# Feed-forward up-projection: one 512-column matmul for both parts of the operand, the two sums added at read-out

## The chip, the core and the metric

The kernel runs on one core of a Trainium2 chip. The core has a matrix engine (PE, TensorE) that writes into PSUM (8 banks of 512 fp32 columns on 128 partitions), a vector engine (DVE), a scalar engine (ACT), a general one (POOL) and a queue (SP) that issues the weight transfers. Each engine works through its own instructions in order and waits on semaphores for the others. The metric is the device time of one execution in microseconds; lower is better.

## The reference

Two stacks of transformer-like layers on 256 tokens of width 1024: four layers (a mixer, cross attention, feed-forward, each with a layer norm) and two more (a mixer with memory attention, feed-forward, with RMS norms). Each of the six has the same kind of feed-forward stage, the part that matters here:

```
def causal_depthwise_conv(x, w, b):      # 3 taps along the sequence
    k_width = w.shape[0]
    s = x.shape[1]
    xp = jnp.pad(x, ((0, 0), (k_width - 1, 0), (0, 0)))
    y = xp[:, 0:s] * w[0]
    for k in range(1, k_width):
        y = y + xp[:, k:k + s] * w[k]
    return y + b

def conv_glu_ffn(x, w_up, conv_w, conv_b, w_down):   # w_up 1024 x 5632, w_down 2816 x 1024
    h = causal_depthwise_conv(x @ w_up, conv_w, conv_b)
    g, u = jnp.split(h, 2, axis=-1)
    return (jax.nn.silu(g) * u) @ w_down
```

The second stack's `conv_ffn` is the same with the halves exchanged. All is fp32.

## The kernel before

PE takes fp32r operands here, so every fp32 matrix is split into a high part (rounded to fp32r) and a low part (the remainder, fp32r again), and a product is three matmuls: high x high, high x low, low x high (`product`, L495). Activations lie transposed, features on partitions, as `xt[0]` (high) and `xt[1]` (low), each 8 tiles of 128 features x 256 tokens.

Weights stream in as 639 units of 128x1024 through a ring of 6 slots. For each unit ACT casts the raw weights to `w_hi` (L1027) and DVE subtracts to make `w_lo` (L1438). Both engines do this in `units`, which stands at fixed places of their programs and runs up to 4 units ahead of the unit in use. A cast waits until PE has used the unit six before.

A feed-forward stage has FT = 22 tiles q. A tile of up-projection is two units (128 features of each half), each 8 k-steps of `product` with the weight as the stationary and 256 tokens as the moving operand: 48 matmuls of 256 columns. Both halves of a tile share one PSUM bank, 4 for even and 6 for odd tiles (the first tile uses 4 and 5). From the third tile on PE follows each up-projection by the down-projection of tile q-2: 12 matmuls of 512 columns into banks 0 to 3 (L909), on the hidden tile in a high and a low part.

Between the two stands a round of ACT and DVE for each tile, both in program order:

- ACT (`tile`, L1346): casts of `units` (three from the third tile on), wait for the up-projection, two bias operations `qt = scale * sum + bias` (L1355, which is also the last of the three taps), SiLU (L1360) after DVE's taps of that half, `hid_hi` (L1365) after DVE's product.
- DVE (`tile`, L1880): the splits of the same units, wait for ACT's bias operations, four tap operations that read PSUM shifted by one or two tokens and add to `qt` (L1892), the product `kt` (L1901), `hid_lo` (L1904) after `hid_hi`.

The round begins again with ACT's cast after `hid_hi`. The bank of a tile is freed by the last tap operation. The order on each engine is that of the program; nothing is scheduled at build time.

Of the kernel before, what the change touches and what calls it, by code (L numbers as in the profile page):

```python
# [10 lines left out]
P = 128  # L11
# [82 lines left out]
class Memory:  # L94
    def __init__(self, nc, ctx, t):
# [4 lines left out]
        self.psum = ctx.enter_context(nc.psum_tensor("psum", [P, 8, BANK], F32))  # L100
        self.x_tok = sbuf("x_tok", [P, TB, D])
        self.n_tok = sbuf("n_tok", [P, TB, D])
        self.xt = [sbuf(f"xt_{part}", [P, KT, SEQ], F32R) for part in ("hi", "lo")]
        self.hid = [sbuf(f"hid_{part}", [P, 2, SEQ], F32R) for part in ("hi", "lo")]
        self.fresh = sbuf("fresh", [P, 2, 2, SEQ])
        self.gain_row = sbuf("gain_row", [P, D])
# [363 lines left out]
class Tensor(Engine):  # L470
# [24 lines left out]
    def product(self, out, stat, mov, first, last):  # L495
# [2 lines left out]
        self.eng.matmul(out, stat[0], mov[1], start=False, stop=False)  # L498
        return self.eng.matmul(out, stat[1], mov[0], start=False, stop=last)  # L499

    def operand(self, j, tb=slice(0, SEQ)):
        self.wait_ge("ready", self.x, j)
        return [x[:, j, tb] for x in self.m.xt]
# [376 lines left out]
    def feed_forward(self, params, silu_half):  # L880
        m = self.m
        bank = (4, 6)

        def up_tile(q):
            if q == 0:

                for k in (4, 5):
                    self.claim(k)
                units = [self.take(KT, P) for _ in range(2)]
                for k in range(KT):  # L890
                    for (hi, lo), b in zip(units, (4, 5)):
                        ins = self.product(m.psum[:, b, 0:SEQ], (hi[:, k, :], lo[:, k, :]), self.operand(k),
                                           k == 0, k == KT - 1)
                        if k == KT - 1:
                            self.used(ins, "made", self.tag, q)
            else:
                self.claim(bank[q % 2])
                for half in range(2):
                    self.used(self.feature_out(m.pair(bank[q % 2])[:, half, :], self.take(KT, P)),
                              "made", self.tag, q)  # L900
            self.free[bank[q % 2]] = ("conv", self.tag, q)
            if q == 0:
                self.free[5] = ("conv", self.tag, q)

        def down_part(q, unit, b, c, last):
            cs, tb = slice(c * BANK, (c + 1) * BANK), slice(b * P, (b + 1) * P)
# [111 lines left out]
class Scalar(Splitter):  # L1018
# [323 lines left out]
    def feed_forward(self, params, silu_half):  # L1342
# [2 lines left out]

        def tile(q):  # L1346
            s = q % 2
            out = [m.pair((4, 6)[s])[:, half, :] for half in range(2)]
            if q == 0:
                out = [m.psum[:, 4, 0:SEQ], m.psum[:, 5, 0:SEQ]]  # L1350
            self.wait_ge("made", self.tag, q)
            if q >= 2:
                self.wait_ge("prod", self.tag, q - 2)
            for half in range(2):
                ins = self.eng.activation(m.qt[:, 2 * s + half, :], out[half], ACT.Identity,  # L1355
                                          scale=col((TAPS - 1) * 2 * FT + half * FT + q),
                                          bias=col(TAPS * 2 * FT + half * FT + q))
            self.up(ins, "base", self.tag, q)
            self.wait_ge("gate_conv", self.tag, q)
            self.up(self.eng.activation(m.kt[:, s, :], m.qt[:, 2 * s + silu_half, :], ACT.Silu),  # L1360
                    "silu", self.tag, q)
            self.wait_ge("prod", self.tag, q)
            if q >= 2:
                self.wait_ge("down", self.tag, q - 2)
            self.up(self.eng.copy(m.hid[0][:, s, :], m.kt[:, 2 + s, :]), "hid_hi", self.tag, q)  # L1365
# [66 lines left out]
class Vector(Splitter):  # L1432
# [443 lines left out]
    def feed_forward(self, params, silu_half):  # L1876
# [2 lines left out]

        def tile(q):  # L1880
            s = q % 2
            out = [m.pair((4, 6)[s])[:, half, :] for half in range(2)]
            if q == 0:
                out = [m.psum[:, 4, 0:SEQ], m.psum[:, 5, 0:SEQ]]
            self.wait_ge("base", self.tag, q)
            first = []
            for d in range(1, TAPS):
# [305 lines left out]
```

## Time and profile before

| what | value |
|---|---|
| median of 3 runs | 2376.48 us (2375.91 to 2378.72) |
| profiled execution, its time | 2377.84 us |
| its span, first to last instruction | 2376.5 us |
| PE busy | 2130.2 us (90%) |
| DVE busy | 1615.2 us (68%) |
| ACT busy | 1217.9 us (51%) |
| matmuls | 13752 |
| mean granted PE clock | 0.945 of 2.4 GHz |

The profile is one execution. Matmuls overlap, so the distance between the starts of two of them, not their duration, is what one costs in a stream. "Idle before" names what released the engine. The line numbers are those of the kernel before.

### The profile page before, as it was taken

Reading aid. Unit: us, or ns where it says so; the run is one execution under the profiler, and the core shown is the slowest. Engines: PE = TensorE matmul, PEld = TensorE weight load, DVE = VectorE, ACT = ScalarE, POOL = GpSimd, SP = SyncE. Lnnn points to the kernel's source line nnn. Section 1 sums busy time; section 2 is a strip of 40 time slices with the busy share of each in tenths; the row PEclk is TensorE's granted clock in tenths of the full one; section 3 lists DMA queues with packets and bytes.
Section 4 is the critical chain, followed back from the end, with each engine's and each line's share of the span. In section 5 each row is a group of like instructions: output and inputs, shape, how many; then the busy total and the mean of one; then the engine's idle time right before and its main releaser. Section 6 shows DMA issues by size and latency. Waiting matters only on the chain.

```text
span 2376.5 us, 34303 instructions
## 1 busy us (share of the span) xinstructions
PE 2130.2 (90%) x13752; PEld 1932.7 (81%) x13752; DVE 1615.2 (68%) x2639; ACT 1217.9 (51%) x2105; POOL 180.3 (8%) x165
## 2 busy tenths in 40 slices
PE   8878899897899979889988787999788999888998
PEld 7757799796789978779987576998777999767997
DVE  4665777787577777577777656776565776766776
ACT  4444455483365555345545444554544655555554
POOL 3001200202010020220001012000000000000000
PEclk9998999898999989899998998999898999999999
DMA  9313566454366643346643134665422766423662
GB/s 286 123 54 113 157 195 185 122 166 140 111 184 187 178 130 124 124 128 200 186 161 128 54 129 144 188 186 151 138 81 86 209 186 185 136 89 116 199 187 94
DMA packets 435454, 352.90 MB, mean 148 GB/s; under 512 B 15869, under 2 KB 381750, under 8 KB 435296
## 3 DMA queue, kind: packets, MB, share of 16 engines
q1 hardware_dynamic: 429296, 332.49, 46.3%
q0 software_dynamic: 6000, 18.22, 2.2%
q8 instruction: 109, 1.79, 0.3%
q14 instruction: 49, 0.40, 0.1%
HBM read 349.62 MB, written 1.05 MB: 148 GB/s over the span
## 4 chain that ended last, share of the span: by engine, by line
PE 77%; DVE 12%; ACT 5%; issue 4%; POOL 1%; DMA 1%; ACTq 0%; SPq 0%; DVEq 0%; POOLq 0%
PE psum L497 19%; PE psum L498 18%; PE psum L499 18%; PE psum L909 14%; PE psum L815 2%; PE psum L802 2%; DVE xt_lo L1453 2%; DVE w_lo L1438 1%; DVE stat L1729 1%; DVE n_tok L1816 1%; PE psum L772 1%; DVE e L1724 1%; ACT xt_hi L1087 1%; POOL norm L2013 1%; ACT w_hi L1027 1%
## 5 line engine op out<-in xcount | busy, mean ns | idle before, releaser
L1438 DVE TENSOR_TENSOR w_lo<-w_raw,w_hi 128x1024 fp32r<-128x1024 f32 x639 | 751.4, 1224 | 193.8 <-ACT w_hi L1027 193.1
L497 PE MATMUL psum<-xt_hi,w_hi 128*128 128x256 f32 x2744 | 794.5, 290 | 70.2 <-ACT xt_hi L1087 50.3
L498 PE MATMUL psum<-xt_lo,w_hi 128*128 128x256 f32 x2744 | 791.7, 289 | 0.0
L499 PE MATMUL psum<-xt_hi,w_lo 128*128 128x256 f32 x2744 | 790.9, 288 | 0.0
L1027 ACT CAST w_hi<-w_raw 128x1024 fp32r<-128x1024 f32 x639 | 645.1, 1047 | 97.0 <-PE psum L499 71.9
L497 PEld LDWEIGHTS psum<-xt_hi,w_hi 128*128 128x128 f32 x2744 | 542.6, 198 | 81.0 <-ACT xt_hi L1087 54.5
L498 PEld LDWEIGHTS psum<-xt_lo,w_hi 128*128 128x128 f32 x2744 | 542.6, 198 | 4.4
L499 PEld LDWEIGHTS psum<-xt_hi,w_lo 128*128 128x128 f32 x2744 | 542.1, 198 | 0.0
L1892 DVE SCALAR_TENSOR_TENSOR qt<-psum,par,qt 128x255 f32<-128x255 f32 (+1 forms) x528 | 218.1, 476 | 152.1 <-ACT qt L1355 151.8
L497 PE MATMUL psum<-w_hi,xt_hi 128*128 128x512 f32 (+4 forms) x700 | 255.9, 366 | 20.5 <-ACT xt_hi L1087 11.6
L498 PE MATMUL psum<-w_lo,xt_hi 128*128 128x512 f32 (+4 forms) x700 | 253.3, 362 | 0.0
L499 PE MATMUL psum<-w_hi,xt_lo 128*128 128x512 f32 (+4 forms) x700 | 253.0, 361 | 0.0
L1355 ACT ACTIVATE qt<-psum,par 128x256 f32<-128x256 f32 x264 | 134.5, 560 | 197.4 <-PE psum L499 197.2
L909 PE MATMUL psum<-w_hi,hid_hi 128*128 128x512 f32 x528 | 207.7, 393 | 4.8 <-DVE hid_lo L1904 4.8
L909 PE MATMUL psum<-w_lo,hid_hi 128*128 128x512 f32 x528 | 207.0, 392 | 0.0
L909 PE MATMUL psum<-w_hi,hid_lo 128*128 128x512 f32 x528 | 205.4, 389 | 0.0
L2013 POOL TENSOR_TENSOR norm<-norm,eps_pow 128x1 f32<-128x1 f32 (+1 forms) x38 | 22.5, 592 | 2125.2 <-DVE norm L1806 1407.9
L497 PEld LDWEIGHTS psum<-w_hi,xt_hi 128*128 128x128 f32 x700 | 134.8, 193 | 42.4 <-ACT xt_hi L1087 12.5
L1078 ACT ACTIVATE fresh<-psum,par 128x256 f32<-128x256 f32 x71 | 35.7, 527 | 241.6 <-PE psum L566 184.7
L499 PEld LDWEIGHTS psum<-w_hi,xt_lo 128*128 128x128 f32 x700 | 134.9, 193 | 19.3
L498 PEld LDWEIGHTS psum<-w_lo,xt_hi 128*128 128x128 f32 x700 | 134.9, 193 | 18.7
L1360 ACT ACTIVATE kt<-qt 128x256 f32<-128x256 f32 x132 | 55.2, 418 | 182.2 <-DVE qt L1892 182.1
(223 smaller groups left out, 2197.5 us busy)
## 6 DMA issues: line engine op xcount, KB each, us to landing
w_raw<-in_f_w_up_dram SPq DMA_DIRECT2D x176, 512.0 KB, 5.1
w_raw<-in_f_w_down_dram SPq DMA_DIRECT2D x88, 512.0 KB, 5.0
w_raw<-in_w_up_dram SPq DMA_DIRECT2D x88, 512.0 KB, 4.9
w_raw<-in_w_down_dram SPq DMA_DIRECT2D x44, 512.0 KB, 5.1
w_raw<-in_x_w_q_dram SPq DMA_DIRECT2D x32, 512.0 KB, 4.6
w_raw<-in_x_w_o_dram SPq DMA_DIRECT2D x32, 512.0 KB, 4.9
w_raw<-in_a_w_qkv_dram SPq DMA_DIRECT2D x24, 512.0 KB, 4.6
w_raw<-in_w_in_fox_dram SPq DMA_DIRECT2D x20, 512.0 KB, 4.9
```

What stands on the lines that cost most here:

```text
L497: self.eng.matmul(out, stat[0], mov[0], start=first, stop=False)
L498: self.eng.matmul(out, stat[0], mov[1], start=False, stop=False)
L499: return self.eng.matmul(out, stat[1], mov[0], start=False, stop=last)
L802: ins = self.eng.transpose(m.psum[:, k, cols.start + b * P - q0:cols.start + (b + 1) * P - q0], m.e[:, g % 2, i, keys[b].start + c * P:key ...
L815: ins = self.eng.matmul(m.psum[p0:p0 + wide, k, slot * SEQ + q0:(slot + 1) * SEQ], vals(c), m.pt[:, g % 2, i, cols], start=c == 0, stop=c ...
L909: ins = self.eng.matmul(m.psum[:, 2 * b + c, :], stat[x], unit[y][:, 0, cs], start=False, stop=last and x == 1, skip_group_check=True)
L1027: self.up(self.eng.copy(self.m.hi[:, s, :], self.m.raw[:, s, :]), "w_hi", u)
L1355: ins = self.eng.activation(m.qt[:, 2 * s + half, :], out[half], ACT.Identity, scale=col((TAPS - 1) * 2 * FT + half * FT + q), bias=col(TA ...
L1360: self.up(self.eng.activation(m.kt[:, s, :], m.qt[:, 2 * s + silu_half, :], ACT.Silu), "silu", self.tag, q)
L1438: self.up(self.eng.tensor_tensor(self.m.lo[:, s, :], self.m.raw[:, s, :], self.m.hi[:, s, :].bitcast(F32), ALU.subtract), "w_lo", u)
L1453: n = self.up(self.eng.tensor_tensor(dst, src, hi.bitcast(F32), ALU.subtract), "ready", (tag, what), j)
L1892: ins = self.eng.scalar_tensor_tensor(cv[:, d:SEQ], out[half][:, 0:SEQ - d], col((TAPS - 1 - d) * 2 * FT + half * FT + q), cv[:, d:SEQ], A ...
```

## The change

Both parts of the operand move into one tile with the high and the low part of each k-tile side by side, so that they are one moving operand of 512 columns. The high part of the weight multiplies both in one matmul, which leaves two sums in one bank: the first 256 columns hold high x high, the other 256 high x low. The low part of the weight multiplies the operand's high part and adds to the first 256 columns. Each half of a tile now has a bank of its own (4 and 5, or 6 and 7). At read-out ACT copies the second sum of each half to SBUF (`low_part`), DVE adds the two sums into SBUF (`whole`), and both ACT's bias operations and DVE's taps read that instead of PSUM. The banks are freed by the adds.

```
+        self.xt_parts = sbuf("xt", [P, KT, 2, SEQ], F32R)
+        self.xt = [self.xt_parts[:, :, part, :] for part in range(2)]
...
+    def product_both(self, k, stat, j, first, last):
+        self.wait_ge("ready", self.x, j)
+        both = self.m.xt_parts[:, j]
+        self.eng.matmul(self.m.pair(k), stat[0], both, start=first, stop=False, skip_group_check=True)
+        return self.eng.matmul(self.m.pair(k)[:, 0, :], stat[1], both[:, 0, :], start=False, stop=last,
+                               skip_group_check=True)
...
         def up_tile(q):
+            ks = [bank[q % 2] + half for half in range(2)]
+            for k in ks:
+                self.claim(k)
+                self.free[k] = ("whole", self.tag, q)
...
             else:
-                self.claim(bank[q % 2])
-                for half in range(2):
-                    self.used(self.feature_out(m.pair(bank[q % 2])[:, half, :], self.take(KT, P)),
-                              "made", self.tag, q)
-            self.free[bank[q % 2]] = ("conv", self.tag, q)
+                for b in ks:
+                    hi, lo = self.take(KT, P)
+                    for k in range(KT):
+                        ins = self.product_both(b, (hi[:, k, :], lo[:, k, :]), k, k == 0, k == KT - 1)
+                    self.used(ins, "made", self.tag, q)
...
# ACT
-            out = [m.pair((4, 6)[s])[:, half, :] for half in range(2)]
+            out = [m.qt[:, 4 + 2 * s + half, :] for half in range(2)]
             self.wait_ge("made", self.tag, q)
             if q >= 2:
                 self.wait_ge("prod", self.tag, q - 2)
+            for half in range(2):
+                ins = self.eng.copy(m.kt[:, 4 + 2 * s + half, :], m.pair(4 + 2 * s + half)[:, 1, :])
+            self.up(ins, "low_part", self.tag, q)
+            self.wait_ge("whole", self.tag, q)
...
# DVE
-            out = [m.pair((4, 6)[s])[:, half, :] for half in range(2)]
+            out = [m.qt[:, 4 + 2 * s + half, :] for half in range(2)]
+            self.wait_ge("low_part", self.tag, q)
+            for half in range(2):
+                ins = self.eng.tensor_tensor(out[half], m.pair(4 + 2 * s + half)[:, 0, :],
+                                             m.kt[:, 4 + 2 * s + half, :], ALU.add)
+            self.up(ins, "whole", self.tag, q)
             self.wait_ge("base", self.tag, q)
```

What each engine has in a row for the third tile (q = 2) of the first stage. ACT before, from the casts to the next cast (L1355 are the bias operations):

```order
L1027 CAST w_hi<-w_raw 128x1024 [waits w_landed0]
L1027 CAST w_hi<-w_raw 128x1024 [waits w_landed1]
L1027 CAST w_hi<-w_raw 128x1024 [waits w_used,w_landed2]
L1355 ACTIVATE qt<-psum,par 128x256 [waits w_used]
L1355 ACTIVATE qt<-psum,par 128x256
```

ACT after (L1365 are now the copies, L1369 the bias operations, L1374 SiLU, L1379 `hid_hi`):

```order
L1039 CAST w_hi<-w_raw 128x1024 [waits w_landed0]
L1039 CAST w_hi<-w_raw 128x1024 [waits w_landed1]
L1039 CAST w_hi<-w_raw 128x1024 [waits w_used,w_landed2]
L1365 COPY kt<-psum 128x256 [waits w_used]
L1365 COPY kt<-psum 128x256
L1369 ACTIVATE qt<-qt,par 128x256 [waits whole]
L1369 ACTIVATE qt<-qt,par 128x256
L1374 ACTIVATE kt<-qt 128x256 [waits gate_conv]
L1379 CAST hid_hi<-kt 128x256 [waits w_used,prod]
```

The two copies took the place of the bias operations behind PE's signal, and the bias operations moved behind a wait for DVE. DVE at the same tile, before:

```order
L1438 TENSOR_TENSOR w_lo<-w_raw,w_hi 128x1024 [waits w_hi] x3
L1892 SCALAR_TENSOR_TENSOR qt<-psum,par,qt 128x255 [waits base]
L1892 SCALAR_TENSOR_TENSOR qt<-psum,par,qt 128x255
L1892 SCALAR_TENSOR_TENSOR qt<-psum,par,qt 128x254 [waits vec] x2
L1901 TENSOR_TENSOR kt<-kt,qt 128x256 [waits conv,silu]
L1904 TENSOR_TENSOR hid_lo<-kt,hid_hi 128x256 [waits hid_hi]
```

and after (L1899 are the adds, L1909 the taps):

```order
L1452 TENSOR_TENSOR w_lo<-w_raw,w_hi 128x1024 [waits w_hi] x3
L1899 TENSOR_TENSOR qt<-psum,kt 128x256 [waits low_part]
L1899 TENSOR_TENSOR qt<-psum,kt 128x256
L1909 SCALAR_TENSOR_TENSOR qt<-qt,par 128x255 [waits base]
L1909 SCALAR_TENSOR_TENSOR qt<-qt,par 128x255
L1909 SCALAR_TENSOR_TENSOR qt<-qt,par 128x254 [waits vec] x2
L1918 TENSOR_TENSOR kt<-kt,qt 128x256 [waits conv,silu]
L1921 TENSOR_TENSOR hid_lo<-kt,hid_hi 128x256 [waits hid_hi]
```

Two adds with a wait for ACT went in ahead of the wait for the bias operations.

## Rows read from the trace of the kernel before

**Rows 1.** The page's part 1: busy time, share of span, instructions.
```profile
PE 2130.2 (90%) x13752; PEld 1932.7 (81%) x13752; DVE 1615.2 (68%) x2639; ACT 1217.9 (51%) x2105; POOL 180.3 (8%) x165
```

**Rows 2.** Windows, of tiles in the first feed-forward stage and of cross attention.
```profile
core 0: us, PE busy (x) PEld busy (x) DVE busy (x) ACT busy (x) POOL busy (x), PEclk, DMA share, GB/s
298.00:445.00 147.00, 147.00 (x1043) 138.66 (x1042) 104.03 (x156) 83.89 (x122) 0.00 (x0) 1.00 0.62 185
606.00:660.00 54.00, 43.15 (x198) 34.85 (x197) 29.88 (x49) 19.05 (x37) 10.24 (x6) 0.93 0.25 69
```

**Rows 3.** PE's timeline over a tile: start us, us, line, operation.
```profile
293.73 0.40 PE L909 MATMUL psum<-w_hi,hid_hi 128*128 128x512 f32 x1
...
296.48 0.28 PE L497 MATMUL psum<-xt_hi,w_hi 128*128 128x256 f32 x1
...
302.23 0.40 PE L909 MATMUL psum<-w_hi,hid_hi 128*128 128x512 f32 x1
```

**Rows 4.** ACT's timeline of a tile in the middle of the stage.
```profile
297.52 3.14 ACT L1027 CAST w_hi<-w_raw 128x1024 fp32r<-128x1024 f32 x3
302.44 1.02 ACT L1355 ACTIVATE qt<-psum,par 128x256 f32<-128x256 f32 x2 [1.77 <-PE psum L499]
```

**Rows 5.** DVE's timeline of the same tile.
```profile
298.59 3.50 DVE L1438 TENSOR_TENSOR w_lo<-w_raw,w_hi 128x1024 fp32r<-128x1024 f32 x3 [0.52 <-ACT w_hi L1027]
303.49 1.65 DVE L1892 SCALAR_TENSOR_TENSOR qt<-psum,par,qt 128x255 f32<-128x255 f32 x4 [1.40 <-ACT qt L1355]
```

**Rows 6.** DVE's timeline at the start of the first stage.
```profile
270.22 4.63 DVE L1438 TENSOR_TENSOR w_lo<-w_raw,w_hi 128x1024 fp32r<-128x1024 f32 x4 [0.26 <-ACT w_hi L1027]
274.97 1.66 DVE L1892 SCALAR_TENSOR_TENSOR qt<-psum,par,qt 128x255 f32<-128x255 f32 x4
...
277.63 0.43 DVE L1904 TENSOR_TENSOR hid_lo<-kt,hid_hi 128x256 fp32r<-128x256 f32 x1 [0.47 <-ACT hid_hi L1365]
...
284.46 3.50 DVE L1438 TENSOR_TENSOR w_lo<-w_raw,w_hi 128x1024 fp32r<-128x1024 f32 x3 [0.53 <-ACT w_hi L1027]
287.87 1.65 DVE L1892 SCALAR_TENSOR_TENSOR qt<-psum,par,qt 128x255 f32<-128x255 f32 x4
...
291.48 3.50 DVE L1438 TENSOR_TENSOR w_lo<-w_raw,w_hi 128x1024 fp32r<-128x1024 f32 x3 [0.53 <-ACT w_hi L1027]
```

**Rows 7.** ACT's timeline of the third tile, beside rows 6.
```profile
283.38 2.94 ACT L1027 CAST w_hi<-w_raw 128x1024 fp32r<-128x1024 f32 x3
286.23 1.01 ACT L1355 ACTIVATE qt<-psum,par 128x256 f32<-128x256 f32 x2
```

**Rows 8.** Prices: DVE's timeline, groups by shape (busy us, mean ns), ACT's timeline.
```profile
87.00 0.41 DVE L1523 TENSOR_TENSOR swap<-psum,rope_sin 128x256 f32<-128x256 f32 x1
87.33 0.41 DVE L1524 TENSOR_TENSOR swap<-psum,rope_sin 128x256 f32<-128x256 f32 x1
...
L1438 DVE TENSOR_TENSOR w_lo<-w_raw,w_hi 128x1024 fp32r<-128x1024 f32 x639 | 751.4, 1224 | 193.8 <-ACT w_hi L1027 193.1
L1525 DVE TENSOR_TENSOR tok<-tok,swap 128x256 f32<-128x256 f32 x12 | 5.1, 425 | 0.4
L1522 DVE TENSOR_TENSOR tok<-psum,rope_cos 128x256 f32<-128x256 f32 x12 | 5.0, 420 | 0.4 <-PE psum L499 0.3
...
L1278 ACT ACTIVATE e<-e,stat 128x256 f32<-128x256 f32 x64 | 31.5, 493 | 0.0
L1278 ACT ACTIVATE e<-psum,stat 128x256 f32<-128x256 f32 x48 | 22.2, 477 | 19.9 <-DVE stat L1737 19.9
L1033 ACT COPY v<-psum 128x256 f32<-128x256 f32 x8 | 2.6, 377 | 12.0 <-PE psum L499 12.0
...
510.41 1.71 ACT L1171 ACTIVATE pt<-v,small 128x256 f32<-128x256 f32 x4
```

**Rows 9.** DVE's timeline: last tile of the first, first and last of the fifth stage.
```profile
450.64 0.42 DVE L1904 TENSOR_TENSOR hid_lo<-kt,hid_hi 128x256 fp32r<-128x256 f32 x1 [0.47 <-ACT hid_hi L1365]
...
1843.38 0.43 DVE L1904 TENSOR_TENSOR hid_lo<-kt,hid_hi 128x256 fp32r<-128x256 f32 x1 [0.47 <-ACT hid_hi L1365]
...
2014.54 0.42 DVE L1904 TENSOR_TENSOR hid_lo<-kt,hid_hi 128x256 fp32r<-128x256 f32 x1 [0.47 <-ACT hid_hi L1365]
```

**Rows 10.** PE's timeline at the end of the first stage.
```profile
451.12 0.50 PE L909 MATMUL psum<-w_hi,hid_hi 128*128 128x512 f32 x1 [0.80 <-DVE hid_lo L1904]
```

More of the change, by code:

```diff
@@ L58 @@
     "base",
+    "low_part",
     "silu", "hid_hi",
@@ L71 @@
     "vec",
+    "whole",
     "gate_conv", "conv", "prod", "hid", "final",
@@ L102, in __init__ @@
         self.n_tok = sbuf("n_tok", [P, TB, D])
-        self.xt = [sbuf(f"xt_{part}", [P, KT, SEQ], F32R) for part in ("hi", "lo")]
+        self.xt_parts = sbuf("xt", [P, KT, 2, SEQ], F32R)
+        self.xt = [self.xt_parts[:, :, part, :] for part in range(2)]
         self.hid = [sbuf(f"hid_{part}", [P, 2, SEQ], F32R) for part in ("hi", "lo")]
@@ L884, in up_tile @@
         def up_tile(q):
+            ks = [bank[q % 2] + half for half in range(2)]
+            for k in ks:
+                self.claim(k)
+                self.free[k] = ("whole", self.tag, q)
             if q == 0:
-                for k in (4, 5):
-                    self.claim(k)
                 units = [self.take(KT, P) for _ in range(2)]
                 for k in range(KT):
-                    for (hi, lo), b in zip(units, (4, 5)):
-                        ins = self.product(m.psum[:, b, 0:SEQ], (hi[:, k, :], lo[:, k, :]), self.operand(k),
-                                           k == 0, k == KT - 1)
+                    for (hi, lo), b in zip(units, ks):
+                        ins = self.product_both(b, (hi[:, k, :], lo[:, k, :]), k, k == 0, k == KT - 1)
                         if k == KT - 1:
@@ L896, in up_tile @@
             else:
-                self.claim(bank[q % 2])
-                for half in range(2):
-                    self.used(self.feature_out(m.pair(bank[q % 2])[:, half, :], self.take(KT, P)),
-                              "made", self.tag, q)
-            self.free[bank[q % 2]] = ("conv", self.tag, q)
-            if q == 0:
-                self.free[5] = ("conv", self.tag, q)
+                for b in ks:
+                    hi, lo = self.take(KT, P)
+                    for k in range(KT):
+                        ins = self.product_both(b, (hi[:, k, :], lo[:, k, :]), k, k == 0, k == KT - 1)
+                    self.used(ins, "made", self.tag, q)
         def down_part(q, unit, b, c, last):
@@ L1347, in tile @@
             s = q % 2
-            out = [m.pair((4, 6)[s])[:, half, :] for half in range(2)]
-            if q == 0:
-                out = [m.psum[:, 4, 0:SEQ], m.psum[:, 5, 0:SEQ]]
+            out = [m.qt[:, 4 + 2 * s + half, :] for half in range(2)]
             self.wait_ge("made", self.tag, q)
@@ L1881, in tile @@
             s = q % 2
-            out = [m.pair((4, 6)[s])[:, half, :] for half in range(2)]
-            if q == 0:
-                out = [m.psum[:, 4, 0:SEQ], m.psum[:, 5, 0:SEQ]]
+            out = [m.qt[:, 4 + 2 * s + half, :] for half in range(2)]
[4 more added lines that the diff above has]
+            self.up(ins, "whole", self.tag, q)
             self.wait_ge("base", self.tag, q)
```

## The prediction

> **What bounds the kernel now.** I read the page's busy shares first: PE is busy for 2130 of 2376.5 us, the other engines much less [rows 1]. An average says little about the six feed-forward stages, so next come the windows. Over 147 us in the middle of the first one PE is busy all the time at a granted clock of 1.00 (its upper level, 2.4 GHz), DVE for 104.0 and ACT for 83.9 us [rows 2]. PE's timeline shows the same tile by tile: 12 down-projection matmuls of 512 columns from 293.73 to 296.48, then 48 up-projection matmuls of 256 columns until 302.23, with no gap [rows 3]. That is 2.75/12 = 0.229 us for 512 columns and 5.75/48 = 0.120 us for 256, and 8.50 us a tile. ACT sits idle for 1.77 us waiting for PE before it reads a tile [rows 4], and DVE then waits 1.40 us for ACT [rows 5]. So each tile ends when PE does.
>
> The start of the same stage shows the second limit. There PE is ahead (the first two tiles carry no down-projection), DVE has no such wait, and its tiles follow at 291.48 - 284.46 = 7.02 us [rows 6]. This is what the round between DVE and ACT costs by itself: three splits, four tap operations, the product, the low part of the hidden tile, and ACT's operations between them. The slack between the two limits is 8.50 - 7.02 = 1.48 us a tile. I expect the change to use up more than that, so it is to be judged on this round, not on PE.
>
> **PE's part.** Per tile, 16 pairs of 256-column matmuls become 16 matmuls of 512 columns; the other 16 of 256 columns stay. Columns are unchanged; what goes is a weight load and the fixed share of a matmul, 2 x 0.120 - 0.229 = 0.011 us each [rows 3]. PE's tile becomes 16 x (0.229 + 0.120) + 2.75 = 8.33 us, a gain of 0.17. Two banks per tile are claimed instead of one; both are freed after the two adds, before the taps, where they used to be held until after the taps, so no new wait comes from there. The new layout of the operand changes strides, not sizes, of the writes of its two parts; I cost it at nothing (these writes come before the loop of tiles).
>
> **ACT's part.** New are two copies of 128x256 out of PSUM, before the two bias operations. A copy of this size takes 0.377 us [rows 8]; two in a row some 0.7. In the start regime ACT's three casts begin at 283.38 and its bias operations at 286.23 [rows 7], while DVE's taps begin at 287.87 [rows 6]. A wait-free ACT would thus finish the copies by 286.95, about 0.9 us before DVE has ended its splits. They are hidden there, and cost nothing. What would expose them is a tile that PE finishes late, and by the sum below PE is not late. Queued behind the copies is ACT's wait for the adds; that delays nothing that DVE is not itself delaying.
>
> **DVE's part, and the new wait.** Two adds of 128x256 (PSUM and SBUF in, SBUF out) stand between the splits and the taps. Two such operations out of PSUM follow each other at 87.33 - 87.00 = 0.33 us and the second takes 0.41 [rows 8]: 0.74 us. Only then may ACT start the two bias operations. They used to run while DVE was still splitting; now DVE stands and waits for them. Their price: 1.02 us for the pair when they read PSUM [rows 4]; now they read SBUF. Exponentials of 256 elements took 0.493 us from SBUF and 0.477 from PSUM [rows 8], so I add 0.02 each: 1.06. Each handoff costs what lies between the end of ACT's pair, 302.44 + 1.02 = 303.46, and DVE's start, 303.49 [rows 4, 5]: 0.03, twice. The taps now read SBUF instead of PSUM; a DVE operation on 256 elements took 0.420 us from PSUM and 0.425 from SBUF [rows 8], so they stay at 1.65.
>
> Added to the round: 0.74 + 0.03 + 1.06 + 0.03 = **1.86 us**. The round becomes 7.02 + 1.86 = 8.88 us, above PE's 8.33, so DVE and ACT set the pace and PE gets to wait about 0.55 us a tile. It will wait before the second half of a tile's up-projection, since that weight's split is the first in DVE's batch of three and the one on which PE has the least lead.
>
> **The sum.** The first tile: DVE ended its splits at 270.22 + 4.63 = 274.85 and its taps began at 274.97 [rows 6]. The new taps begin at 274.85 + 1.86 = 276.71: 1.74 later. The second tile carries two splits; a split is (3.50 - 1.22)/2 = 1.14 us in a row of them [rows 5, 8], so its round was 7.02 - 1.14 = 5.88 and becomes 7.74. Twenty more rounds follow at 8.88: 177.6. From the old start of the first hid_lo to the new start of the last: 1.74 + 7.74 + 177.6 = 187.1 us. Before, this was 450.64 - 277.63 = 173.0 in the first stage and 2014.54 - 1843.38 = 171.2 in the fifth, which is the shortest [rows 6, 9]; the others took 172.5 to 173.0, and the six together are 1035.4. What PE does after the last hid_lo (it waited 0.80 us for it and then had the last seven groups to do [rows 10]) is the same in both kernels. Sum: 6 x 187.1 - 1035.4 = **+87 us**. The profiled execution took 2377.8 against the median's 2376.5; from the median this gives **2463.5 us**, 3.7% slower.
>
> Ends for the unknowns. Low: bias pair as two scaled operations from SBUF in a row of four, 1.71 us for four, which is 0.41 + 0.49 = 0.90 [rows 8]; taps at the 0.33 pitch of plain operations, 3 x 0.33 + 0.41 = 1.40, or 0.25 less; added 1.45, round 8.47, six stages 6 x (1.33 + 7.33 + 169.4) = 1068, so +33 us: 2409.5. High: adds without overlap 0.84, bias pair without overlap 1.12, added 2.02, round 9.04, six stages 1143.6, so +108 us: 2485.
>
> **Rivals.** *Shorter taps.* DVE might read SBUF faster than PSUM. The rows speak against it (0.420 and 0.425 [rows 8]), but none is of this operation. With 0.25 us less per tile the round is 8.63, a stage 1.49 + 7.49 + 172.6 = 181.6, and the time 2376.5 + 6 x 181.6 - 1035.4 = 2431. The Trainium skill, VectorE: DVE Perf Modes, in the section on the TRN2 errata, has 58 fixed cycles for VectorE from SBUF against 120 from PSUM, and 224 against 172 for ScalarE. By that rule, an estimate: four taps save 4 x 62 cycles at 0.96 GHz, 0.26 us, and the two bias operations lose 0.09; on ACT's pair of 1.02 the added time is 0.74 + 0.06 + 1.11 - 0.26 = 1.65, the round 8.67, and the time about 2436. The durations in rows 8 bear out the second half in sign and not the first.
>
> *PE stays the bound, and the kernel is faster.* If the round stayed under PE's 8.33, the 0.17 us would be gained on 132 tiles: -23 us, 2353. It decides at the round: no change in the time needs 6 x (22c - 8.28) = 1035.4 with c the round, which is c = 8.22, or 1.20 us added where I have 1.86. The adds and two handoffs are 0.80; the bias pair would have to take 0.4 us with unchanged taps. Even the low end, 1.45, does not reach it. Against it too: the 7.02 us rounds with which each stage starts are lost whatever PE does.
>
> *The 512-column matmul doesn't save its share.* If the two sums in one bank cost PE as much as before, PE's tile stays at 8.50, still under 8.88, and the time is the forecast's. This matters only beside the low end.
>
> *PE's clock falls.* PE now pauses in every tile. In the window of cross attention it was busy for 43 of 54 us and still had 0.93 of the clock [rows 2]; with 94% busy I expect 1.00. If it fell to the lower level in a stretch, PE's tile would double there, about 8 us lost per tile so hit; one tile a stage gives +50 on top, 2510.
>
> **Chances.** Forecast (rounds 8.75 to 9.05) 0.63, shorter taps 0.18, PE remains the bound 0.06, between that and no change 0.05, clock or another stall 0.08. The range has to hold forecast, shorter taps and both ends: 2405 to 2490. A measurement here can tell about 0.2% from no change. Faster by over 0.2% 0.06, within 0.2% 0.04, slower 0.90.
>
> **What would show it.** DVE's timeline: adds right behind the splits without a wait on the copies, then an idle stretch of about 1.12 us for ACT's bias operations in every tile, and hid_lo at 8.88 us from the third tile on instead of 7.0 and then 8.50. ACT: no wait for PE before the copies, a wait for the adds instead. PE: a pause of some 0.55 us a tile for the split weights, 0.349 us for a pair of 512 and 256 columns. It would be wrong if the copies showed up as what DVE waits for, if the bias pair took well under 1 us, or if PE had no pause.

## The result, and the profile after

| what | before | changed kernel |
|---|---|---|
| median on the same chip | 2376.30 us | 2480.66 us (2478.77 to 2481.71, 4 runs) |
| ratio | | 1.0436, 95% interval 1.0418 to 1.0454 |
| profiled execution: its span | 2376.5 us | 2479.2 us |
| mean granted PE clock | 0.945 | 0.935 |

The kernel is 4.4% slower. The forecast was 2463.5 us, 3.7% slower, with a range of 2405 to 2490.

The page's part 1 of the changed kernel, to be read beside [rows 1]:

```profile
PE 2159.2 (87%) x11640; PEld 1824.2 (74%) x11640; DVE 1706.8 (69%) x2903; ACT 1290.2 (52%) x2369; POOL 180.3 (7%) x165
```

PE has 2112 instructions fewer and yet is busy for 29 us more. That is no work: matmuls overlap, so a pause shows as idle time only once the last record has ended. The first matmul after a pause has a longer record (0.50 us instead of 0.40, below), and where the clock is low every record is longer (0.63 us, below). The chain of work that ended last has changed owner. The page's part 4 of the kernel before:

```profile
PE 77%; DVE 12%; ACT 5%; issue 4%; POOL 1%; DMA 1%; ACTq 0%; SPq 0%; DVEq 0%; POOLq 0%
```

and of the changed kernel:

```profile
DVE 42%; PE 32%; ACT 18%; issue 6%; POOL 1%; DMA 1%; ACTq 0%; SPq 0%; DVEq 0%; POOLq 0%
```

The window over the middle of the first feed-forward stage, as in [rows 2] (columns: window, us, then PE, weight load, DVE, ACT, POOL busy with instructions, granted clock, DMA share, GB/s), and one over the end of that stage:

```profile
298.00:445.00 147.00, 142.20 (x725) 117.47 (x726) 109.64 (x180) 86.98 (x149) 0.00 (x0) 1.00 0.59 178
466.00:474.00 8.00, 7.37 (x21) 5.57 (x21) 7.21 (x12) 1.44 (x2) 0.56 (x1) 0.69 0.23 67
```

In the middle PE was busy for all 147 us before; now it is idle for 4.8 us of them, at the same full clock. It is starved there, not slowed. (4.8 us in 147/8.95 = 16.4 tiles are 0.29 each; by the starts of the matmuls a pause is longer.)

DVE's timeline of the changed kernel, from the first tile of the first stage and then a tile in the stage; it answers [rows 5] and [rows 6]:

```profile
269.39 4.63 DVE L1452 TENSOR_TENSOR w_lo<-w_raw,w_hi 128x1024 fp32r<-128x1024 f32 x4 [0.25 <-ACT w_hi L1039]
...
275.86 1.67 DVE L1909 SCALAR_TENSOR_TENSOR qt<-qt,par 128x255 f32<-128x255 f32 x4 [1.16 <-ACT qt L1369]
277.98 0.43 DVE L1918 TENSOR_TENSOR kt<-kt,qt 128x256 f32<-128x256 f32 x1 [0.46 <-ACT kt L1374]
278.88 0.43 DVE L1921 TENSOR_TENSOR hid_lo<-kt,hid_hi 128x256 fp32r<-128x256 f32 x1 [0.47 <-ACT hid_hi L1379]
...
286.69 0.43 DVE L1921 TENSOR_TENSOR hid_lo<-kt,hid_hi 128x256 fp32r<-128x256 f32 x1 [0.47 <-ACT hid_hi L1379]
287.64 3.50 DVE L1452 TENSOR_TENSOR w_lo<-w_raw,w_hi 128x1024 fp32r<-128x1024 f32 x3 [0.52 <-ACT w_hi L1039]
291.05 0.75 DVE L1899 TENSOR_TENSOR qt<-psum,kt 128x256 f32<-128x256 f32 x2
292.97 1.67 DVE L1909 SCALAR_TENSOR_TENSOR qt<-qt,par 128x255 f32<-128x255 f32 x4 [1.16 <-ACT qt L1369]
...
296.59 3.50 DVE L1452 TENSOR_TENSOR w_lo<-w_raw,w_hi 128x1024 fp32r<-128x1024 f32 x3 [0.52 <-ACT w_hi L1039]
```

One round is 296.59 - 287.64 = 8.95 us. The adds follow the splits with no wait on the copies. Then DVE is idle for 1.16 us, released by ACT's bias operations. From the adds' start to the taps' start it is 292.97 - 291.05 = 1.92 us, which was nothing before; from the taps to the next splits it is 296.59 - 292.97 = 3.62, against 291.48 - 287.87 = 3.61 in [rows 6]. So the whole addition sits at that one place. The second tile's hid_lo comes 286.69 - 278.88 = 7.81 us after the first's.

ACT's timeline at the same tile, which answers [rows 4] and [rows 7]:

```profile
289.42 0.63 ACT L1365 COPY kt<-psum 128x256 f32<-128x256 f32 x2
291.84 1.09 ACT L1369 ACTIVATE qt<-qt,par 128x256 f32<-128x256 f32 x2 [1.79 <-DVE qt L1899]
```

The copies end at 289.42 + 0.63 = 290.05, a full 1.00 us before DVE's adds begin. The bias pair now waits 1.79 us for DVE, where it waited 1.77 for PE in [rows 4].

PE's timeline at a tile in the middle, which answers [rows 3]:

```profile
321.39 0.39 PE L510 MATMUL psum<-xt,w_hi 128*128 128x512 f32 x1
...
324.71 0.50 PE L510 MATMUL psum<-xt,w_hi 128*128 128x512 f32 x1 [0.35 <-DVE w_lo L1452]
...
327.59 0.39 PE L921 MATMUL psum<-w_hi,hid_hi 128*128 128x512 f32 x1
```

The up-projection takes 327.59 - 321.39 = 6.20 us with one pause in the middle, before the second half's first matmul, for the split weight. Eight pairs without a pause took 327.59 - 324.71 = 2.88 us (a first one that starts slower included).

Four operations by their source lines (engine, operation, count, duration in ns as least/median/most). The taps and the bias operations of the kernel before:

```profile
L1892 DVE SCALAR_TENSOR_TENSOR qt<-psum,par,qt x528: 469/474/486, 275.0 to 2360.6; 128x255 f32<-128x255 f32 x88, 128x254 f32<-128x254 f32 x88
...
L1355 ACT ACTIVATE qt<-psum,par x264: 547/558/568, 273.9 to 2358.9; 128x256 f32<-128x256 f32 x132
```

and of the changed kernel, with the copies, what they waited for and what waited for them:

```profile
L1909 DVE SCALAR_TENSOR_TENSOR qt<-qt,par x528: 474/479/486, 275.9 to 2461.4; 128x255 f32<-128x255 f32 x88, 128x254 f32<-128x254 f32 x88
...
L1369 ACT ACTIVATE qt<-qt,par x264: 584/596/607, 274.7 to 2459.6; 128x256 f32<-128x256 f32 x132
...
L1365 ACT COPY kt<-psum x264: 355/368/381, 272.9 to 2457.3; 128x256 f32<-128x256 f32 x132
its engine sat idle before it (us, times) until:
  PE psum L511: 3.4, 3
who waited for it (us, times):
  DVE qt L1899: 0.7, 1
```

Taps from SBUF take 479 ns against 474 from PSUM, bias operations 596 against 558. The copies waited for PE in 3 of 132 tiles, 3.4 us in all. DVE's adds waited for the copies once, 0.7 us, in the first tile of the last stage; there the sums come late in the kernel before too (DVE waited 1.13 us for the bias operations).

**The sum against the spans.** The changed span is 102.7 us longer. The six stretches from a stage's first hid_lo to its last were 1035.4 us and are now 1118.1 (186.7 five times and 184.5 in the last stage), which is +82.7. The first round of each lasts 7.80 to 7.82, the other twenty 8.93 to 8.96; the exception is the final round of the last stage, 6.66, where no weights are left to split. The other +20.0 us lie between the stages: from a last hid_lo to the next first one, and the two ends of the kernel. The forecast had 6 x (7.74 + 177.6) - 1035.4 = +76.6 for the first and 6 x 1.74 = +10.4 for the second.

PE's timeline at the end of the first stage, which answers [rows 10]:

```profile
458.92 0.47 PE L921 MATMUL psum<-w_hi,hid_hi 128*128 128x512 f32 x1 [3.11 <-DVE w_lo L1452]
...
466.06 0.80 PE L921 MATMUL psum<-w_hi,hid_hi 128*128 128x512 f32 x1 [6.21 <-DVE hid_lo L1921]
466.66 0.63 PE L921 MATMUL psum<-w_lo,hid_hi 128*128 128x512 f32 x1
467.08 0.63 PE L921 MATMUL psum<-w_hi,hid_lo 128*128 128x512 f32 x1
...
473.04 0.40 PE L921 MATMUL psum<-w_hi,hid_lo 128*128 128x512 f32 x1
```

Before, PE waited 0.80 us for the last hid_lo; now it waits 3.11 and 6.21 us, and then its matmuls of 512 columns start 467.08 - 466.66 = 0.42 us apart instead of 0.23, until 470.92. The granted clock of that window is 0.69 (above): the lower level, 1.2 GHz, for its first half. The last of these 21 matmuls starts 7.46 us after hid_lo where it was 5.15 before; over the six stages it starts 13.0 us later in all (1.6 to 2.8 each). In the other stages the first wait is 3.1 to 3.2 us too, and the second is 5.5 to 6.0, in the last stage 3.25.

### The profile page after: what moved, and what is told of

It is laid out like the page before. It is cut to its first block, busy times and chain, and to the rows that moved or that the text cites. A ratio compares the mean times of both kernels' runs of the same rounds, so it can differ in the third digit from the quotient of the medians.

```text
span 2479.2 us, 30607 instructions
## 1 busy us (share of the span) xinstructions
PE 2159.2 (87%) x11640; PEld 1824.2 (74%) x11640; DVE 1706.8 (69%) x2903; ACT 1290.2 (52%) x2369; POOL 180.3 (7%) x165
## 4 chain that ended last, share of the span: by engine, by line
DVE 42%; PE 32%; ACT 18%; issue 6%; POOL 1%; DMA 1%; ACTq 0%; SPq 0%; DVEq 0%; POOLq 0%
DVE w_lo L1452 19%; PE psum L501 8%; PE psum L502 7%; PE psum L503 7%; DVE qt L1909 7%; ACT w_hi L1039 6%; ACT qt L1369 6%; DVE qt L1899 3%; DVE kt L1918 2%; ACT kt L1374 2%; PE psum L828 2%; DVE xt L1467 2%; PE psum L815 2%; PE psum L921 1%; DVE stat L1743 1%
## 5 line engine op out<-in xcount | busy, mean ns | idle before, releaser
L510 PE MATMUL psum<-xt,w_hi 128*128 128x512 f32 x2112 | 775.6, 407 | 63.7 <-DVE w_lo L1452 38.5
L511 PE MATMUL psum<-xt,w_lo 128*128 128x256 f32 x2112 | 596.8, 283 | 0.0
L510 PEld LDWEIGHTS psum<-xt,w_hi 128*128 128x128 f32 x2112 | 403.3, 191 | 191.7 <-DVE w_lo L1452 64.7
L511 PEld LDWEIGHTS psum<-xt,w_lo 128*128 128x128 f32 x2112 | 405.0, 192 | 4.4
L1909 DVE SCALAR_TENSOR_TENSOR qt<-qt,par 128x255 f32<-128x255 f32 (+1 forms) x528 | 220.1, 479 | 153.5 <-ACT qt L1369 153.5
L501 PE MATMUL psum<-w_hi,xt 128*128 128x512 f32 (+4 forms) x700 | 256.4, 366 | 21.1 <-ACT xt L1099 11.6
L1369 ACT ACTIVATE qt<-qt,par 128x256 f32<-128x256 f32 x264 | 144.5, 594 | 238.9 <-DVE qt L1899 238.9
L502 PE MATMUL psum<-w_lo,xt 128*128 128x512 f32 (+4 forms) x700 | 253.6, 362 | 0.0
L503 PE MATMUL psum<-w_hi,xt 128*128 128x512 f32 (+4 forms) x700 | 253.2, 362 | 0.0
L501 PE MATMUL psum<-xt,w_hi 128*128 128x256 f32 x632 | 191.1, 302 | 39.5 <-ACT xt L1099 25.5
L502 PE MATMUL psum<-xt,w_hi 128*128 128x256 f32 x632 | 188.7, 299 | 0.0
L503 PE MATMUL psum<-xt,w_lo 128*128 128x256 f32 x632 | 188.3, 298 | 0.0
L501 PEld LDWEIGHTS psum<-w_hi,xt 128*128 128x128 f32 x700 | 135.2, 193 | 42.7 <-ACT xt L1099 12.5
L501 PEld LDWEIGHTS psum<-xt,w_hi 128*128 128x128 f32 x632 | 131.8, 209 | 43.5 <-ACT xt L1099 27.8
L921 PEld LDWEIGHTS psum<-w_hi,hid_hi 128*128 128x128 f32 x528 | 102.7, 194 | 80.3 <-DVE hid_lo L1921 36.2
```

Source lines behind the costliest of these rows:

```text
L501: self.eng.matmul(out, stat[0], mov[0], start=first, stop=False)
L510: self.eng.matmul(self.m.pair(k), stat[0], both, start=first, stop=False, skip_group_check=True)
L511: return self.eng.matmul(self.m.pair(k)[:, 0, :], stat[1], both[:, 0, :], start=False, stop=last, skip_group_check=True)
L921: ins = self.eng.matmul(m.psum[:, 2 * b + c, :], stat[x], unit[y][:, 0, cs], start=False, stop=last and x == 1, skip_group_check=True)
L1909: ins = self.eng.scalar_tensor_tensor(cv[:, d:SEQ], out[half][:, 0:SEQ - d], col((TAPS - 1 - d) * 2 * FT + half * FT + q), cv[:, d:SEQ], A ...
```

## The experiments

**The two halves of the change apart.** The first kernel has the joined matmul but reads only the first sum, as the kernel before did; the second has the read-out with the matmuls split again.

```
# e1_matmul_alone: ACT and DVE as before, on the first sum alone
-            out = [m.qt[:, 4 + 2 * s + half, :] for half in range(2)]
+            out = [m.pair(4 + 2 * s + half)[:, 0, :] for half in range(2)]
...
-                ins = self.eng.copy(m.kt[:, 4 + 2 * s + half, :], m.pair(4 + 2 * s + half)[:, 1, :])
-            self.up(ins, "low_part", self.tag, q)
-            self.wait_ge("whole", self.tag, q)
...
# e2_readout_alone: 48 matmuls of 256 columns
-        self.eng.matmul(self.m.pair(k), stat[0], both, start=first, stop=False, skip_group_check=True)
+        for part in range(2):
+            self.eng.matmul(self.m.pair(k)[:, part, :], stat[0], both[:, part, :], start=first and part == 0,
+                            stop=False, skip_group_check=True)
```

> PE's part alone: the joined matmuls stay, but the second sum is not read; ACT's bias operations and DVE's taps read the first sum from PSUM as in the kernel before, the banks are freed after the taps (so the product high weight x low operand is left out of the result). Theory A (the round of DVE and ACT costs the time, PE's part saves 0.17 us a tile): tiles at 8.33 us, 132 x 0.176 = 23 us faster than before, 2353 us. Rival B (the joined matmul, the second bank or the new layout of the operand carries part of the loss): at or above 2376 us, tiles at 8.50 us or more.

> The read-out alone: two banks, copies, adds and waits as in the changed kernel, but the joined matmul of 512 columns is issued as two of 256 columns, one into each half of the bank, so that PE's tile is 8.50 us again. Theory A: PE at 8.50 is still under the round of 8.95, so nothing changes against the changed kernel, 2480 us within 3. Rival B (PE's part matters): 0.17 us x 132 = 23 us slower than the changed kernel, 2503 us.

Measured: the matmul alone 2366.51 us, ratio 0.9953 (0.9938 to 0.9968); the read-out alone 2478.96 us, 1.0428 (1.0413 to 1.0444). The same window of the first:

```profile
298.00:445.00 147.00, 147.00 (x774) 125.39 (x774) 105.57 (x158) 84.90 (x123) 0.00 (x0) 1.00 0.63 188
```

and of the second:

```profile
298.00:445.00 147.00, 144.27 (x999) 133.36 (x998) 110.23 (x180) 87.99 (x149) 0.00 (x0) 1.00 0.59 174
```

With the matmul alone PE is busy for the whole window, and a round takes 8.38 to 8.39 us: the joined matmul saves 0.11 us a tile, 14.1 us in the six stretches (1021.3 against 1035.4). In the time only 9.9 us of that arrive; no run shows where the rest goes. With the read-out alone the rounds are 8.95, the same as in the changed kernel, though 2.73 us of the 147 are left idle instead of 4.80. So the whole loss is the read-out's, and what the matmul saves is not seen beside it. My 2353 for the first was too low: the saving is smaller than my 0.17, and three or four of the 21 rounds of a stage, those at its start, never wait for PE.

**The bias operations taken out of the path.** They read the first sum from PSUM as before, beside the splits; the adds stay on DVE.

```
-            out = [m.qt[:, 4 + 2 * s + half, :] for half in range(2)]
+            out = [m.pair(4 + 2 * s + half)[:, 0, :] for half in range(2)]      # ACT
...
-            self.up(ins, "low_part", self.tag, q)
-            self.wait_ge("whole", self.tag, q)
...
-            self.wait_ge("low_part", self.tag, q)                               # DVE
+            self.wait_ge("base", self.tag, q)
```

> All work of the changed kernel stays, but ACT's two bias operations read the first sum from PSUM straight behind the copies and do not wait for DVE's adds (so the product high weight x low operand is missing from the last tap); DVE's adds wait for the bias operations instead, and the taps follow the adds. Theory A (what costs is that DVE stands while ACT makes the bias operations, 1.16 us a tile, beside 0.75 us of adds): round 8.95 - 1.16 + 0.05 = 7.8 us, under PE's 8.33, so PE is the bound again and the time is about 2355 to 2360 us. Rival C (the two adds and the two copies as work are what costs, the order is not): near 2480 us, at least above 2430.

Measured: 2374.03 us (2370.65 to 2377.25), 0.9988 (0.9978 to 0.9997). DVE's timeline of a tile:

```profile
293.72 3.50 DVE L1450 TENSOR_TENSOR w_lo<-w_raw,w_hi 128x1024 fp32r<-128x1024 f32 x3 [0.53 <-ACT w_hi L1039]
297.14 0.75 DVE L1897 TENSOR_TENSOR qt<-psum,kt 128x256 f32<-128x256 f32 x2
297.92 1.67 DVE L1908 SCALAR_TENSOR_TENSOR qt<-qt,par 128x255 f32<-128x255 f32 x4
...
301.54 2.36 DVE L1450 TENSOR_TENSOR w_lo<-w_raw,w_hi 128x1024 fp32r<-128x1024 f32 x2 [0.52 <-ACT w_hi L1039]
```

The round is 301.54 - 293.72 = 7.82 us: the adds stay at 0.75, the 1.16 us of idle time are gone, and later in each stage PE sets 8.39. ACT's pair behind DVE's adds is thus worth 1.13 us a tile by itself, and without that wait the time is about that of before (this kernel leaves high x low out of the last tap). The time is above the expected 2355 to 2360. The stretches sum to 1021.9 us, which is 13.5 less than before, where 16 to 21 were expected of the time, since PE's tile is 8.39 and not 8.33, and part of that is lost again between the stages. PE's timeline at the end of the first:

```profile
448.89 0.50 PE L921 MATMUL psum<-w_hi,hid_hi 128*128 128x512 f32 x1 [2.16 <-DVE hid_lo L1920]
```

The wait is 2.16 us instead of 0.80, the granted clock of 448 to 456 us is 0.79, and in four of the six stages the last matmul starts 6.74 to 6.78 us after hid_lo instead of 5.15.

**The price of the adds, and of the copies.** Each is done twice, the extra result going to a spare tile.

```
# e5_adds_twice, on DVE
+                self.eng.tensor_tensor(m.v[:, s, half * SEQ:(half + 1) * SEQ], m.pair(4 + 2 * s + half)[:, 0, :],
+                                       m.kt[:, 4 + 2 * s + half, :], ALU.add)
# e7_copies_twice, on ACT
+                self.eng.copy(m.v[:, s, half * SEQ:(half + 1) * SEQ], m.pair(4 + 2 * s + half)[:, 1, :])
```

> The changed kernel with DVE's two adds issued twice (the first pair into a spare tile). A dose of one of the two terms. Theory A (everything DVE does in the round counts in full): 2 x 0.33 = 0.67 us more a tile, round 9.61 us, 132 tiles: 88 us above the changed kernel, 2569 us. Rival D (part of the adds is cover for the wait on ACT or on PE): well under 88 us more.

> The changed kernel with ACT's two copies out of PSUM issued twice (the first pair into a spare tile), 0.55 us more work for ACT a tile. Theory A says that the copies end about 1.0 us before DVE has its splits, so that another 0.55 us hides too: 2480 us within 3. Rival F (the copies are on the path): 132 x 0.55 = 73 us more, 2553 us.

Measured: adds twice 2567.41 us, 1.0799 (1.0784 to 1.0813), with rounds of 9.61 us; copies twice 2481.26 us, 1.0436 (1.0422 to 1.0451), with rounds of 8.95. DVE's timeline with the adds doubled:

```profile
299.63 3.49 DVE L1452 TENSOR_TENSOR w_lo<-w_raw,w_hi 128x1024 fp32r<-128x1024 f32 x3 [0.53 <-ACT w_hi L1039]
303.04 0.75 DVE L1899 TENSOR_TENSOR v<-psum,kt 128x256 f32<-128x256 f32 x2
303.71 0.74 DVE L1902 TENSOR_TENSOR qt<-psum,kt 128x256 f32<-128x256 f32 x2
...
309.23 2.36 DVE L1452 TENSOR_TENSOR w_lo<-w_raw,w_hi 128x1024 fp32r<-128x1024 f32 x2 [0.53 <-ACT w_hi L1039]
```

and ACT's with the copies doubled:

```profile
299.97 0.63 ACT L1365 COPY v<-psum 128x256 f32<-128x256 f32 x2
300.50 0.65 ACT L1367 COPY kt<-psum 128x256 f32<-128x256 f32 x2
302.39 1.09 ACT L1371 ACTIVATE qt<-qt,par 128x256 f32<-128x256 f32 x2 [1.25 <-DVE qt L1901]
```

0.67 us more of adds lengthens the round by 0.66; 0.53 us more of copies lengthens nothing, it only shortens ACT's wait for DVE from 1.79 to 1.25 us. The path and its cover are where the prediction put them.

**The ends of the stages.** PE gets 24 matmuls on a tile of zeros, into a bank that is free there, before its last wait for hid_lo; in the second kernel also 12 before the wait for the split weights. The third is the changed kernel again, on the same chip as the second.

```
# e9_both_waits_filled; e6_end_filled has the second loop alone, with its own claim
+        self.claim(4)
+        for _ in range(12):
+            self.eng.matmul(m.psum[:, 4, :], m.zeros[:, 0:P], m.zeros[:], start=True, stop=True, skip_group_check=True)
         units = [self.take(1, D) for _ in range(2)]
...
+                    if (b, c, q) == (0, 0, FT - 1):
+                        for _ in range(24):
+                            self.eng.matmul(m.psum[:, 4, :], m.zeros[:, 0:P], m.zeros[:], start=True, stop=True,
+                                            skip_group_check=True)
                     self.wait_ge("hid", self.tag, q)
```

> The changed kernel with 24 extra matmuls of 512 columns on zeros into the free bank 4 at the end of each stage, where PE waits 6.2 us for the last hidden tile and its clock then falls to 1.2 GHz for the first 11 of 21 down-projection matmuls (0.43 against 0.23 us). Theory E (the wait lets the clock fall, and that carries part of the about 8 us between the stages that the rounds don't explain): the 21 matmuls take 4.8 instead of 7.2 us, and 5 to 8 us less than the changed kernel in all, about 2474 us; granted clock up. If the clock there doesn't matter, or falls all the same: 2480 us. The extra matmuls take 5.5 us, so that they end before the hidden tile is there.

> The changed kernel with both waits of PE at the end of a stage filled: 12 extra matmuls of 512 columns on zeros (2.75 us at 0.229) in the wait of 3.2 us for the split weights of the last down-projection, and 24 (5.5 us) in the wait of 6.2 us for the last hidden tile. In the earlier run with 24 in the second wait alone, the clock had fallen in the first one, the 24 took 7.0 us and the last group began 1.2 to 3.3 us after hid_lo instead of 0.48. Theory E (it is the fallen clock that makes the last 21 matmuls end late): now they begin at 0.48 and the last one starts 5.2 us after hid_lo, as in the kernel before, against 6.7 to 8.0 in the changed kernel, and the time is 5 to 8 us below the changed kernel run beside it, about 2473 us. If the clock falls all the same, or nothing hangs on these matmuls: the same time as the changed kernel.

> The changed kernel as it is, on the same chip as the run beside it: 2480 us within 2. It serves as the measure for the run with both waits filled.

Measured: one wait filled 2477.77 us, 1.0422 (1.0407 to 1.0436); both filled 2475.50 us (2475.25 to 2475.85), 1.0415 (1.0401 to 1.0429); the changed kernel again 2481.30 us (2478.97 to 2481.78), 1.0437 (1.0423 to 1.0451). PE's timeline with one wait filled:

```profile
459.18 0.47 PE L921 MATMUL psum<-w_hi,hid_hi 128*128 128x512 f32 x1 [3.18 <-DVE w_lo L1457]
...
460.19 7.01 PE L941 MATMUL psum<-zeros 128*128 128x512 f32 x24
```

and with both:

```profile
456.18 2.91 PE L936 MATMUL psum<-zeros 128*128 128x512 f32 x12
...
460.30 5.65 PE L943 MATMUL psum<-zeros 128*128 128x512 f32 x24
466.68 0.50 PE L921 MATMUL psum<-w_hi,hid_hi 128*128 128x512 f32 x1 [0.73 <-DVE hid_lo L1928]
```

With one wait filled the clock had fallen in the first wait already (24 in 7.01 us, 0.29 each), so the filling itself ran late and held up the real work by 0.5 to 2.8 us in each stage. Even so the last matmuls of the stages start 5.9 us earlier in all than with the copies doubled, on the same chip, and the time is 3.5 us below that run's 2481.26 (2475.89 to 2479.52 against 2480.01 to 2482.45). With both filled the 24 take 5.65 us (0.235 each), the granted clock of 466 to 474 us is 1.00 instead of 0.69, the last matmul starts 5.15 to 5.19 us after hid_lo in five of six stages (6.43 in the sixth), and the time is 5.8 us below that of the changed kernel beside it, with no overlap of the runs. The last matmuls start 11.7 us earlier in all than in the changed kernel beside it. So idle waits ahead of the last group cost the clock, and that costs about 6 us of the time. In both runs about half of what the last matmuls gained shows in the time (3.5 of 5.9 and 5.8 of 11.7 us); no run shows where the rest is absorbed.

**A better place for the sums.** Copies and adds move ahead of the casts and splits, so that ACT can do its bias operations while DVE splits. In the first kernel this holds for tiles 2 to 20; in the second, tiles 2 to 17 are joined this way and the first two and last four tiles have the three matmuls and the read-out of the kernel before (the operand's layout and a bank for each half stay).

```
# e4_sums_first, on ACT and on DVE
+            early = 2 <= q < FT - 1
+            if early:
+                read_out(q)              # the copies, or the adds
             self.units(3 if q >= 2 else 2)
+            if not early:
+                read_out(q)
             tile(q)
...
# e8_middle_tiles
+def joined(q):
+    return 2 <= q < 18
...
+        if not joined:
+            return self.product(self.m.pair(k)[:, 0, :], stat, self.operand(j), first, last)
...
+            if joined(q):
+                read_out(q)
             self.units(3 if q >= 2 else 2)
```

> The changed kernel in another order, from the third tile to the last but one of a stage: ACT's copies of a tile stand ahead of the three casts and DVE's adds ahead of the three splits, where PE has the tile ready anyway, so that the bias operations run beside the splits. Theory A: round of DVE and ACT about 7.7 us (one copy pair 0.63 us more than the 7.02 of before), below PE's 8.33, so tiles at 8.33 us. The last tile keeps its order and its hidden tile comes 1.5 us later than before, 9 us in six stages: 2376 - 23 + 9 = 2362 us. Rival C (the work itself costs): DVE has the same operations as the changed kernel, so 2430 us or more. Rival B: PE's tile above 8.33 and the time above 2376.

> Joined matmuls with the sums first (as in the run before with that order) only in tiles 2 to 17 of a stage; the first two and the last four tiles are the three-matmul form of before with its read-out, so that a stage starts as before and DVE has made up its lag by the end. Theory A with what the earlier runs showed (PE's joined tile is 8.39 us against 8.50, and the loss lay in the last tile, whose hidden tile came 8.45 us after its sums against 4.16, and in the fallen clock behind that): 16 x 6 x 0.115 = 11 us faster than before, 2365 us. If the loss lies in the middle tiles: 2385 us or more.

Measured: sums first 2398.48 us, 1.0089 (1.0072 to 1.0106); middle tiles alone 2371.24 us (2369.95 to 2372.45), 0.9974 (0.9965 to 0.9984). DVE's timeline of a tile with the sums first:

```profile
369.42 0.76 DVE L1907 TENSOR_TENSOR qt<-psum,kt 128x256 f32<-128x256 f32 x2 [0.94 <-ACT kt L1364]
370.37 3.50 DVE L1460 TENSOR_TENSOR w_lo<-w_raw,w_hi 128x1024 fp32r<-128x1024 f32 x3 [0.19 <-ACT w_hi L1039]
373.78 1.66 DVE L1921 SCALAR_TENSOR_TENSOR qt<-qt,par 128x255 f32<-128x255 f32 x4
...
377.81 0.76 DVE L1907 TENSOR_TENSOR qt<-psum,kt 128x256 f32<-128x256 f32 x2 [0.94 <-ACT kt L1364]
```

The taps follow the splits without the idle time, and the round is 377.81 - 369.42 = 8.39 us, PE's (7.57 while PE is ahead). The theory of the round holds, yet the time missed my 2362 by 36 us and is 22 above that of before. The six stretches from first to last hid_lo are 1036.3 us, no better than before, since the first rounds are 7.81 and 7.57 where they were 5.88 and 7.01, and the last is 8.94. By the spans 20 us lie between the stages again, where I had put 9: this kernel's last tile still has the changed order, and PE's row there reads

```profile
452.95 0.79 PE L921 MATMUL psum<-w_hi,hid_hi 128*128 128x512 f32 x1 [5.34 <-DVE hid_lo L1933]
```

with matmuls at the lower clock behind it (granted clock of 452 to 460 us: 0.63). With tiles 2 to 17 alone the end is as before (a wait of 0.80 us, the last matmul after 5.15 to 5.19 us in all stages), the stretches sum to 1024.1 us, 11.3 less than before as expected, and this version beats the kernel before by 0.26%. The time is 6 us above my 2365, since only 6.3 of the 11.3 us arrive in it, as with the matmul alone. Of the 2.9 us by which the stretches are longer than with the matmul alone, the four last tiles at 8.50 instead of 8.39 us explain 6 x 4 x 0.11 = 2.6. Where the form switches there is one long round, of 7.7 to 9.5 us:

```profile
282.29 0.42 DVE L1944 TENSOR_TENSOR hid_lo<-kt,hid_hi 128x256 fp32r<-128x256 f32 x1 [0.47 <-ACT hid_hi L1394]
284.33 0.75 DVE L1916 TENSOR_TENSOR qt<-psum,kt 128x256 f32<-128x256 f32 x2 [1.62 <-ACT kt L1370]
...
291.36 0.42 DVE L1944 TENSOR_TENSOR hid_lo<-kt,hid_hi 128x256 fp32r<-128x256 f32 x1 [0.47 <-ACT hid_hi L1394]
```

Here the casts and splits stand behind a read-out for which PE isn't ready yet, and DVE waits 1.62 us. That costs nothing: in none of the six stages does PE wait for anything from there to its last group. DVE is late by it until, behind tile 17, it makes up the lag in rounds of 7.01 us.

## Why the prediction was right, and where it was off

**The bound moved, as said.** PE's 8.39 us a tile lost to a round of ACT and DVE of 8.95; each half alone and the doubled parts show it. Of the 102.7 us by which the span grew, the forecast's sum accounts for 87.1; of the other 15.6 us, 6.1 are the round and 9.6 lie between the stages.

**The round: 8.95 for 8.88.** The adds took 0.75 (0.74 forecast), the idle time for the bias pair 1.16 (1.12). The mis-sized term is the pair: 1.09 instead of 1.06, since a bias operation that reads SBUF takes 38 ns more than one that reads PSUM (596 against 558), where I took 20 from the exponentials in [rows 8]. The taps, put at no change, grew by 5 ns each. In the six stages this came to 6 x (186.7 - 185.3) less the 2.3 us of the very last round, which I had not seen to be shorter: +6.1 us beside the forecast.

**The copies were hidden**, with 1.00 us of slack where I had 0.9, in all but one tile (0.7 us, above). **PE's pause** stands before the second half's weights, as said: 8.95 - 8.39 = 0.56 us a tile for 0.55, of which the profile names 0.35 as a wait for DVE.

**PE's gain was over-sized.** The pair took 0.352 us instead of 0.349, the tile 8.39 instead of 8.33, the gain 0.11 instead of 0.17. It changed nothing, because PE isn't the bound; in the rival where PE stays the bound it would have: 2366.5 measured for the matmul alone, not 2353. The operand's new layout, which I costed at nothing, shows no cost in its writes: DVE's 69 low parts made from `fresh` average 1114 ns in both kernels, ACT's 69 high parts 613.

**The first tile.** Splits' end to taps' start is 275.86 - 274.02 = 1.84 us against 0.12, so 1.72 later for 1.74. The first stage's first tile has 0.36 more, a wait for ACT's SiLU (277.98 above) that no other stage has: the SiLU ends at 277.58 and the product follows after 0.40 us, where it is 0.04 in the second stage. I don't know its cause.

**What failed** is the sentence that what PE does after the last hid_lo "is the same in both kernels". Between the stages the span grew by 20.0 us, where the first tiles account for 10.4. The last tile's round no longer runs beside PE's work but leaves PE waiting for 3.11 and 6.21 us, the clock falls, and half of the last group runs at the lower level, 1.2 GHz. I had looked for a falling clock in the pauses of the tiles, and priced it there alone. Filling the waits gave 5.8 us back. The first stage's wait for SiLU is 0.36. Some 3.4 us between the stages remain that no run assigns; executions of the kernel before differ by as much (2375.5 to 2379.2 us in these runs). That the time stayed within 2405 to 2490 is in part luck: the high end of 2485 was made of longer adds and a longer bias pair, and the larger part of what was missing, 9.6 of 15.6 us, came from a place to which I had given no range.

**The rivals.** *Shorter taps* falls: 479 ns from SBUF against 474 from PSUM. The rule of the Trainium skill, VectorE: DVE Perf Modes, in the section on the TRN2 errata, by which VectorE has a fixed part of 58 cycles from SBUF and 120 from PSUM, does not show in these operations; its other half, that ScalarE is slower from SBUF, agrees in sign, 38 ns against an estimate of 43 from its cycle counts. *PE stays the bound* falls by the 8.95. *The 512-column matmul doesn't save its share* falls too: it saved 0.11 of 0.17. *PE's clock falls* is wrong for the place that it was priced at, since the pauses in the tiles left the clock at 1.00; it fell at the ends of the stages, for about 1 us each in the time instead of 8.

## What to carry to other kernels

Before a matmul is made cheaper at the price of a longer read-out, work out the round of the engines that read it and compare it with PE's time per tile; here 1.5 us of slack stood against 1.9 us of additions to gain 0.11 us a tile. What an operation adds depends on its place: here the copies cost nothing, while ACT's bias pair, hardly changed in itself, cost 1.13 us a tile once it stood between two of DVE's steps, and only a reordering that put it beside the splits, in the tiles where PE is the bound, made the change pay, by 0.26%. And look at the last tile apart: here its round had no matmuls beside it, and the longer wait cost its own length and the clock after it.

## What the runs showed of the hardware

The clock fell after short waits in an otherwise full stream. After a wait of 0.80 us at a stage's end the last group ran at full speed in all stages (before, matmul alone, middle tiles). After 2.16 us, in the kernel with the early bias operations, four of six stages lost 1.6 us in it. After a single wait of 5.34 us (3.08 in the last stage), with the sums first, all six lost 1.6 to 2.9; after one of 3.1 to 3.2 and, three matmuls later, one of 3.25 to 6.21 us, in the changed kernel, all six lost 1.6 to 2.8. The pauses of 0.56 us in each tile, and of 9.61 - 8.39 = 1.22 us with the adds doubled, left the granted clock of the stage at 1.00. Matmuls of no use, put into both waits, kept it at 1.00 and made the kernel faster by 5.8 us.

A 512-column and a 256-column matmul that alternate cost 0.352 us a pair where three of 256 columns cost 0.359: with one weight load per matmul, joining two of 256 columns saves 7 ns of that.
